# GpSimd's table expansion and first-layer loads moved behind the first input projection of a two-layer trunk kernel

## What is computed

```python
for l in range(DEPTH):                                    # DEPTH = 2
    sh1, sc1, gt1, sh2, sc2, gt2 = silu(c) @ w_ada[l] + b_ada[l]   # 6 x 1024, for c and for c_ctx
    h = rms_norm(z, g_attn[l]) * (1 + sc1) + sh1
    na_q, na_k, na_v, mla_q, ckv, kpe, sw_q, sw_k, sw_v = project(h, w_in[l], g_mla_q[l], w_mla_qb[l], g_mla_kv[l])
    # A) neighbourhood attention, with a learned bias rpb[:, dr, dc] over the row and column distance,
    #    and the cached keys and values of 128 context tokens
    # B) latent attention: keys and values = ckv @ w_mla_kvb, queries = rms_norm(cq) @ w_mla_qb
    # C) windowed attention with a sink logit per head
    z = z + gt1 * (concat(o_na, o_mla, o_swa) @ w_out[l])
    h = rms_norm(z, g_ffn[l]) * (1 + sc2) + sh2
    z = z + gt2 * moe(h, w_router, b_router, w_gate[l], w_up[l], w_down[l])   # 16 experts, top 2 in one group
return rms_norm(z, g_final), ...                          # and the new keys and values of the context
```

## Time and profile before

| | us |
|---|---|
| median of three executions | 1347.58 |
| lowest and highest | 1346.36, 1349.18 |
| profiled execution, its own time | 1345.4 |
| its span, first to last instruction | 1343.5 |
| TensorE busy | 1178.3 (88% of the span) |
| VectorE busy | 777.1 (58%) |
| ScalarE busy | 623.0 (46%) |
| GpSimd busy | 111.8 (8%) |

### The profile page before, as it was taken

One profiled execution on the slowest core, in us unless ns is written; L12 is line 12 of the kernel. 1 busy time (PEld: TensorE's weight loads), 2 busy tenths in 40 slices (PEclk: granted clock), 3 DMA queues, 4 the chain that ended last, 5 costly groups with the idle time before them and its releaser, 6 DMA issues.

```text
span 1343.5 us, 15058 instructions
## 1 busy us (share of the span) xinstructions
PE 1178.3 (88%) x5638; PEld 858.7 (64%) x5638; DVE 777.1 (58%) x1068; ACT 623.0 (46%) x739; POOL 111.8 (8%) x124
## 2 busy tenths in 40 slices
PE   5599887779879999999948998889769999999956
PEld 4266444345467888888836764555467888888846
DVE  1212343341658888988825023572477898888835
ACT  2100233430346777778622003561237777877721
POOL 4000020000010110111001001100010011101000
PEclk8799999999869999999975999899859999999985
DMA  9973377861738999999829233001218999999612
GB/s 261 337 248 117 103 265 250 254 248 63 297 113 317 368 366 372 376 372 378 311 103 276 79 121 94 15 1 58 74 62 303 372 383 369 376 370 369 243 56 97
DMA packets 88702, 310.23 MB, mean 231 GB/s; under 512 B 31272, under 2 KB 35620, under 8 KB 76348
## 3 DMA queue, kind: packets, MB, share of 16 engines
q1 hardware_dynamic: 65548, 279.17, 57.2%
q0 software_dynamic: 11792, 18.65, 4.6%
q10 hardware_dynamic: 11296, 11.54, 2.7%
HBM read 307.07 MB, written 24.27 MB: 247 GB/s over the span
## 4 chain that ended last, share of the span: by engine, by line
PE 78%; DVE 7%; issue 4%; DMA 4%; ACT 4%; ACTq 2%; SPq 1%; POOL 0%; POOLq 0%; DVEq 0%
PE bank L780 15%; PE bank L1011 13%; PE bank L1005 13%; PE bank L1006 13%; DMA ring<-in_w_ada 3%; ACT work L1206 3%; PE bank L762 3%; PE bank L884 2%; PE bank L995 2%; PE bank L787 2%; PE bank L898 2%; PE bank L985 2%; PE bank L707 1%; ACTq L1178 1%; PE bank L831 1%
## 5 line engine op out<-in xcount | busy, mean ns | idle before, releaser
L1680 DVE TENSOR_TENSOR ring_r<-ring,work_r 128x4096 fp32r<-128x4096 f32 x96 | 421.6, 4417 | 5.8 <-ACT work_r L1256 5.6
L1256 ACT ACTIVATE work_r<-ring 128x4096 fp32r<-128x4096 f32 x96 | 348.5, 3632 | 139.7 <-PE bank L1006 120.7
L1005 PE MATMUL bank<-work_r 128*128 128x512 f32 x768 | 311.9, 406 | 21.5 <-ACT work_r L1256 9.6
L1006 PE MATMUL bank<-work_r 128*128 128x512 f32 x768 | 305.0, 397 | 0.0
L780 PE MATMUL bank<-hT,ring 128*128 128x384 f32 (+1 forms) x640 | 213.2, 492 | 5.2 <-ACT hT L1132 3.8
L1011 PE MATMUL bank<-ring_r,work_r 128*128 128x512 f32 x768 | 195.0, 396 | 0.4 <-DVE ring_r L1680 0.4
L1005 PEld LDWEIGHTS bank<-work_r 128*128 128x128 f32 x768 | 148.4, 193 | 53.6 <-issue 19.2
L780 PEld LDWEIGHTS bank<-hT,ring 128*128 128x128 f32 (+1 forms) x640 | 120.8, 191 | 90.3 <-issue 11.4
L1006 PEld LDWEIGHTS bank<-work_r 128*128 128x128 f32 x768 | 148.0, 193 | 29.7
L1011 PEld LDWEIGHTS bank<-ring_r,work_r 128*128 128x128 f32 x768 | 144.2, 188 | 34.7 <-DVE ring_r L1680 0.8
L1104 ACT ACTIVATE work<-bank 128x384 f32<-128x384 f32 (+6 forms) x79 | 37.4, 495 | 198.7 <-PE bank L780 94.1
(11 more groups left out here) (200 smaller groups left out, 1151.3 us busy)
## 6 DMA issues: line engine op xcount, KB each, us to landing
ring<-in_w_gate SPq DMA_DIRECT2D x32, 2048.0 KB, 7.8
ring<-in_w_up SPq DMA_DIRECT2D x32, 2048.0 KB, 10.8
ring<-in_w_down SPq DMA_DIRECT2D x32, 2048.0 KB, 10.4
ring<-in_w_ada SPq DMA_DIRECT2D x24, 2048.0 KB, 8.6
ring<-in_w_in SPq DMA_DIRECT2D x4, 2048.0 KB, 13.5
work<-yscr ACTq DMA_DIRECT2D x12, 512.0 KB, 6.1
ring<-in_w_out SPq DMA_DIRECT2D x4, 1280.0 KB, 8.3
ring<-in_w_in SPq DMA_DIRECT2D x12, 256.0 KB, 8.5
```

Source lines behind the costliest of these rows:

```text
L1005: mm(b[:], x_hi[:, k, :], hi[:, k, half, :], start=(k == 0), stop=False)
L1006: last = mm(b[:], x_lo[:, k, :], hi[:, k, half, :], start=False, stop=False)
L1256: A_(w_hi[:, slot % 2, :], ring[slot][:], ACT.Copy).then_inc(s_hi, 1)
L1680: tt(ring_r[slot][:], ring[slot][:], w_hi[:, slot % 2, :].bitcast(F32), ALU.subtract).then_inc(s_lo, 1)
```

## The change

One wait is added to GpSimd's list. It stands between the wait for the eight small table transfers and the transfer that writes the expanded table. It waits until TensorE has finished `cq0` of the first layer, the first product of the input projection.

```diff
             g.wait_ge(s_bp, 16 * DEPTH * NAH)
+
+            is_filled(g, (0, "cq0"))
             nrow = DEPTH * NAH * DRS
             g.dma_start(bscr.rearrange("r (q c) -> r q c", q=GW), bpad[0:nrow, :].unsqueeze(1).to_broadcast([nrow, GW, TW]))\
                 .then_inc(s_bscr, 16)
```

## The result

The changed kernel took **1326.4 us**, the kernel before 1347.0 us (medians of four executions each, 1325.79 to 1329.72 and 1346.04 to 1349.18). The ratio is 0.985, with a 95% interval of 0.983 to 0.987: faster by 20.6 us, or 1.5%. The profiled execution has a span of 1324.3 us, 19.2 us less than before's 1343.5 us. The forecast was 1329.1 us, a gain of 18.5 us.

What follows compares the result with a forecast made beforehand. The prediction took the first 55 us to be bound by the `w_ada` stream. Its terms, -18.5 + 0 + 0 us from the 1347.6 us median, gave 1329.1 us, range 1326 to 1334 us.

Steps and rivals of the forecast that it cites:

- What bounds the kernel: First 55 us: TensorE waits for the `w_ada` stream, slowed by GpSimd's transfers; no transfer wait from there to `mq`.
- Part 1: Start: without GpSimd's transfers SP's queue runs at 0.382 MB/us, the fourth `w_ada` chunk lands at 36.4 us, gain 18.5 us.
- Part 2: `w_ada` products at the start: mostly at full clock, TensorE is ready at 34.7 us, so the stream still ends last by 1.7 us.
- rival 1: TensorE at half clock in the `w_ada` products: gain only 15.4 or 13.9 us, 1332 to 1334 us; chance 0.13.
- Part 3: GpSimd's wait for `cq0`, due at 49.3 us: `wqb` lands at 80.4 us, 45 us before `mq`; cost 0.
- the priced cover: Between release and `mq`: the projections hide the late transfers, `wqb` landing 45 us and the table 60 us early.
- Part 4: After `cq0`: the moved transfers slow SP's queue, but later chunks still arrive in time; cost 0, up to 18.5 us without cover.
- the slow stretch: Time of low DMA rate beside GpSimd's transfers: moves to about 50 to 76 us, with SP's queue at 0.111 MB/us.
- The sum: Whole kernel: -18.5 us at the start, 0 for the wait and 0 for the collision, giving 1329.1 us.
- rival 2: Stream at the start: removing GpSimd's transfers frees only their bytes' time, 8.4 us, giving 1339 us; chance 0.08.
- rival 3: Whole kernel: the gained time is absorbed later or the early transfers were free, no gain, 1347.6 us; chance 0.04.

Runs made afterwards that it cites:

- Experiment 4: The changed kernel with GpSimd's release moved from `cq0`: to the third `w_in` chunk's last product, 1343.0 us; to the turn of the third `w_ada` chunk, 1326.6 us.
- release_nak1: The changed kernel, but GpSimd waits for the last product of the third `w_in` chunk instead of `cq0`: 1343.0 us, 0.996 of the kernel before.
- experiment 1: Both kernels run again unchanged: the changed kernel 1326.9 us against 1349.2 us for the kernel before, ratio 0.985.
- experiment 3: The kernel before, with table rows of 512 instead of 508 bytes: 1340.3 us; with the table over ScalarE's hardware queue instead: 1340.5 us; before beside them 1348.6 us.

## Why the prediction was right

- **What bounds the kernel.** Right: one transfer term in the chain, and behind it no wait for a transfer up to `mq`.
- **Part 1, the stream.** Forecast: fourth chunk at 36.4 us; measured 37.7 us. The rate was right (387 GB/s; 0.382 MB/us had been taken). The bytes were 0.4 MB short in this profile: SP's queue had moved 12.29 MB by 37.7 us, not 11.90, and it had 4.70 MB at 18 us instead of 4.87. Gain at the fourth product 17.2 instead of 18.5 us. That is scatter: in the other two profiles of the changed kernel the chunk is there at 36.2 and 36.1 us with 11.74 and 11.81 MB moved.
- **Part 2, TensorE's clock.** A mixture of forecast and rival 1. A2 and most of A1 did run at 2.4 GHz (A0 and A1 took 5.80 us together) and the stream did end last (2.64 us of waiting for 1.7 forecast). But A3 fell into a stretch at half clock, behind 2.64 us of standing still, and cost 1.6 us, the price that rival 1 had for it. That stretch comes and goes: in the second and third profile A3 ran at full clock, and the projection started at 42.7 and 42.6 us, for 42.9 us forecast.
- **Part 3, the added wait.** Right in place, off by a few us. Release at 52.8 us, forecast 49.3 (the two terms above, 2.9 us, and 0.6 us until GpSimd had issued). Landing of `wkvb` at 78.3, forecast 80.4. No wait at `mq`. Experiment 4 shows that the priced cover was real: released 59 us later, the landing sets the start of `mq`.
- **Part 4, the collision.** Right that it costs nothing; one term was mis-sized. SP's queue was to get 0.111 MB/us in the slow stretch and got 1.07 MB in 24 us, 0.045 MB/us. Its packets were now 285 bytes on average (3749 of them, `w_in` 3), where they had been 2 KB; beside the table in release_nak1 they were 2 KB again, and it got 0.113 MB/us. So the rate goes with the packets of the stream, by these three. The backlog then ended at about 101 us and not at 92 us, and the pause of the DMA engines paid for that too.
- **The sum.** -18.5 us forecast; -15.6 us at the start in the first pair of profiles, -19.2 us in the span, -20.6 us in the medians. That this span came so near from such a start is luck: the start was outside the forecast's 17 to 21 us, and 3.3 us of clock in the routing, which the prediction had not considered, went the other way. The forecast itself does not rest on that: over all profiles the start gains 19.6 us and the span 19.3 us (experiment 1). The prediction had named the clock as a rival at the start only, and it moves the whole: one kernel gave 1322.2 to 1328.7 us in five executions.
- **The rivals.** "Only the bytes count" (rival 2) is true of the loads (2.1 us of at most 3.7) and false for the table (14.5 us against 4.8). The prediction let the rows of 508 bytes explain the slow stretch; experiment 3 shows that they do it only in the software queue, and not all of it. "Nothing" (rival 3) fell, and with it, for this place, the rule of the Trainium skill to issue transfers early (DMA: Bandwidth & Descriptors, Rules for kernel authors): early was not free where the engines had a stream that TensorE waited on.

## What to carry to other kernels

Before a transfer is issued early because its queue is free, ask what else the DMA engines carry then: at 100% share and six tenths of the usual GB/s, an early transfer is paid by whoever waits for the stream. Look at the size of a row and at the queue before the size of the transfer: here 1.8 MB in rows of 508 bytes over the software queue cost 14.5 us at the start, 1.4 MB of loads 2.1 us, and four bytes more per row gave 6.3 us back. And a few us that a profile shows at one end of a kernel are only real when more executions than one have them; two profiles are compared at the same instructions, not at the same microsecond.

## What the runs showed of the hardware

- Rows of 508 bytes written from the software queue pulled the DMA engines down to 162 GB/s together (122 us of one engine per MB of them); with rows of 512 bytes it was 342 GB/s (50 us per MB, loads included); with no such write beside the stream, 383 to 387 GB/s.
- The same short rows over ScalarE's hardware queue took 54 us of one engine per MB and left the stream 0.263 MB/us instead of 0.111 MB/us, but needed some 33 us for the 1.8 MB.
- Beside the table in the software queue the stream had 0.11 MB/us with packets of 2 KB and 0.045 MB/us with packets of 285 bytes on average.
- Two loads of 3.0 KB, one row of 24 bytes read for 128 partitions, blocked the 16 engines: from 6 to 8 us, 16 packets of 192 bytes took 20.2 us of one engine's time (63% of what the 16 had), and 19 GB/s were moved in all.
- The stretch at half clock in the first layer's routing was 23.9 us in some executions and 30.7 us in others of one and the same kernel, worth about 3 us between two matching instructions (8.8 and 11.9 us).
